# Value rows of four groups summed on TensorE through diagonals, in a block of attention and expert retrieval

## What is computed

```python
def _peer(xn, w_q, sub_keys, u_tab, v_tab):
    def body(xb):                                   # 128 tokens
        q = (xb @ w_q).reshape(128, 8 heads, 2, 128)
        sc = einsum('thpd,hpkd->thpk', q, sub_keys)
        s1, i1 = top_k(sc[:, :, 0], 16); s2, i2 = top_k(sc[:, :, 1], 16)
        top_s, pos = top_k(all 256 sums s1 + s2, 16)
        eidx = i1 * 128 + i2 at pos                 # 16 of 16384 experts
        g = softmax(top_s)
        hid = gelu(einsum('thkd,td->thk', u_tab[eidx], xb)) * g
        return einsum('thk,thkd->td', hid, v_tab[eidx])
h = h + _peer(rmsnorm(h)); out = rmsnorm(h)
```

## Time and profile before

| quantity | value |
|---|---|
| median of three runs | 1542.28 us |
| the profiled execution itself | 1541.62 us |
| its span, first to last instruction | 1539.8 us |
| mean granted TensorE clock | 0.939 of full speed |
| TensorE (PE) matmul busy | 1269.3 us, 82% |
| VectorE (DVE) busy | 1077.6 us, 70% |
| GpSimd (POOL) busy | 751.5 us, 49% |
| ScalarE (ACT) busy | 459.8 us, 30% |
| first dot to last add of the hosted stage | 110.06 to 529.7 us |

### The profile page before, as it was taken

The page is one execution under the profiler, slowest core; times in us unless marked ns, Lnnn a source line. Parts: engine busy times, 40 slices in busy tenths (PEclk is TensorE's granted clock), DMA queues, the critical chain, the costliest instruction groups (busy, mean ns, idle before and its releaser), DMA issues.

```text
span 1539.8 us, 13062 instructions
## 1 busy us (share of the span) xinstructions
PE 1269.3 (82%) x3727; PEld 658.2 (43%) x3727; DVE 1077.6 (70%) x2520; ACT 459.8 (30%) x1200; POOL 751.5 (49%) x637
## 2 busy tenths in 40 slices
PE   9999999988888488999787777677886787777778
PEld 7766655665545234444333333233332233332333
DVE  3247699999988867566666676666666766666654
ACT  3432355466343022222222222221222222222212
POOL 0016477675667443454544554445444554444440
PEclk9999999999989699999899999989999999999998
DMA  9669799997999999999999999999999999999995
GB/s 382 250 250 413 275 330 351 370 376 268 340 371 392 391 421 416 421 421 421 421 422 422 421 422 421 421 422 421 422 421 421 422 422 421 422 420 422 421 421 208
DMA packets 99741, 596.50 MB, mean 387 GB/s; under 512 B 11480, under 2 KB 11480, under 8 KB 42328
## 3 DMA queue, kind: packets, MB, share of 16 engines
q0 software_dynamic: 89856, 536.91, 86.0%
q1 hardware_dynamic: 9816, 58.77, 9.6%
HBM read 593.54 MB, written 2.10 MB: 387 GB/s over the span
## 4 chain that ended last, share of the span: by engine, by line
DMA 42%; PE 15%; DVE 6%; POOL 3%; issue 2%; ACT 2%; DVEq 0%; POOLq 0%
PE acc L994 13%; DMA map_mem<-in_peer_uv_dram,eidx 10%; DMA w_ring<-in_peer_uv_dram,eidx 9%; DMA v_all<-in_peer_uv_dram,eidx 7%; DMA act_mem<-in_peer_uv_dram,eidx 6%; DMA v_ring<-in_peer_uv_dram,eidx 3%; DMA mix_mem<-in_peer_uv_dram,eidx 3%; DMA u_ring<-in_peer_uv_dram,eidx 3%; DMA v_ring<-in_peer_v_dram,eidx 2%; PE mm L786 1%; ACT diag L1228 1%; DVE map_mem L1549 1%; DVE w_ring L1549 1%; PE sc L786 1%; POOL v_ring L692 1%
## 5 line engine op out<-in xcount | busy, mean ns | idle before, releaser
L1220 ACT ACTIVATE gel<-hid 128x4 f32<-128x4 f32 x126 | 25.8, 205 | 722.2 <-DVE hid L1549 712.5
L685 POOL DMA_INDIRECT u_ring<-in_peer_u_dram,eidx x112 | 136.8, 1221 | 172.9 <-DVE eidx L1529 99.5
L994 PE MATMUL acc<-v_all,diag 128*128 128x512 f32 x256 | 129.2, 651 | 61.1 <-ACT diag L1228 60.6
L692 POOL DMA_INDIRECT v_ring<-in_peer_v_dram,eidx x112 | 133.4, 1192 | 66.4 <-DVE h L1577 38.0
L1577 DVE SCALAR_TENSOR_TENSOR h<-v_ring,coef,h 128x1024 f32<-128x1024 f32 x112 | 143.9, 1284 | 14.3 <-DMA v_ring<-in_peer_v_dram,eidx 11.3
L994 PE MATMUL acc<-map_mem,diag 128*128 128x512 f32 x248 | 123.3, 644 | 32.0 <-ACT diag L1228 32.0
L994 PE MATMUL acc<-v_ring,diag 128*128 128x512 f32 x248 | 120.1, 629 | 32.3 <-ACT diag L1228 28.7
L1541 DVE CUSTOM_DVE_ANT_0 u_ring<-u_ring,hn 128x1024 f32<-128x1024 f32 x112 | 136.6, 1220 | 14.2 <-DMA u_ring<-in_peer_u_dram,eidx 14.0
L994 PE MATMUL acc<-u_ring,diag 128*128 128x512 f32 x248 | 119.1, 626 | 27.4 <-ACT diag L1228 25.8
L1228 ACT ACTIVATE diag<-ident,coef 128x128 f32<-128x128 f32 x392 | 126.3, 390 | 39.1 <-DVE coef L1567 30.8
L711 POOL DMA_INDIRECT v_all<-in_peer_uv_dram,eidx x64 | 76.1, 1189 | 92.3 <-PE acc L994 81.7
(11 more groups left out here) (281 smaller groups left out, 2331.9 us busy)
## 6 DMA issues: line engine op xcount, KB each, us to landing
w_ring<-in_slabs_dram SPq DMA_DIRECT2D x29, 1024.0 KB, 8.4
v_ring<-in_slabs_dram SPq DMA_DIRECT2D x6, 1024.0 KB, 11.2
u_ring<-in_slabs_dram SPq DMA_DIRECT2D x6, 1024.0 KB, 10.9
map_mem<-in_slabs_dram SPq DMA_DIRECT2D x6, 1024.0 KB, 7.9
h<-in_x_dram SPq DMA_DIRECT2D x4, 512.0 KB, 12.5
u_ring<-in_peer_u_dram,eidx POOLq DMA_INDIRECT x112, 6.9
v_ring<-in_peer_v_dram,eidx POOLq DMA_INDIRECT x112, 7.1
v_all<-in_x_cols_dram SPq DMA_DIRECT2D x3, 512.0 KB, 7.4
```

The lines of the kernel that those rows point to most:

```text
L685: nc.gpsimd.indirect_dma_start(out=u_ring[:, c % U_RING, :], out_offset=None, in_=peer_u[0], in_offset=bass.IndirectOffsetOnAxis(ap=eidx[n ...
L692: nc.gpsimd.indirect_dma_start(out=v_ring[:, c % V_RING, :], out_offset=None, in_=peer_v[0], in_offset=bass.IndirectOffsetOnAxis(ap=eidx[n ...
L994: last = nc.tensor.matmul(acc[half][:, :], diag[:, c % COLS, :], v_row(n, c)[:, half * BANK:(half + 1) * BANK], start=first, stop=(n % PH ...
L1220: nc.scalar.activation(gel[:, par, g0:g0 + COLS], hid[:, par, g0:g0 + COLS], ACT.Gelu).then_inc(gelu_done, 1)
```

## The change

Groups 5, 9, 13 and 17 (the tuple `SUMMED`) are no longer added row by row on VectorE. ScalarE makes four diagonals of their coefficients in a memory of their own (`sum_diag`, laid over the buffers `z_f` and `e_f` of the forget gate), TensorE multiplies each diagonal with its v row and accumulates the four rows in two banks of the rotation `mm`, one per 512 columns, and VectorE adds the two banks to `h` one slot later, or earlier if an `outproj` comes first. TensorE's part stands at gap 0 of slot k + 2, and the planner leaves room behind it (`SHARE_SUM` = 10.0). The adds of slots 7, 11, 15 and 19 fall away.

```diff
+SUMMED = (5, 9, 13, 17)
+SHARE_SUM = 10.0
...
     total, at = sum(share(p) for p in later), 0.0
+    total += SHARE_SUM * len(SUMMED)
+    summed_at = {(k + BEHIND) * GAPS: ("sum", k) for k in SUMMED}
     for p in later:
         k = int(at / total * (SLOTS - 1) * GAPS)
+        while summed_at and k >= min(summed_at):
+            slot = min(summed_at)
+            AFTER[slot].append(summed_at.pop(slot))
+            at += SHARE_SUM
+            k = int(at / total * (SLOTS - 1) * GAPS)
...
+        def row_taken(i):
+
+            if i // COLS in SUMMED and i % COLS == COLS - 1:
+                return mm_full, mm_done(("sum", i // COLS, 1))
+            return added, i + 1 - sum(COLS * k + COLS - 1 <= i for k in SUMMED)
...
             def gather_v(n, c):
                 if n or c >= V_RING:
-                    pool.wait_ge(added, TOPK * n + c + 1 - V_RING)
+                    pool.wait_ge(*row_taken(TOPK * n + c - V_RING))
...
+                elif kind == "sum":
+                    k, = p
+                    pe.wait_ge(*row_taken(COLS * k - 1))
+                    banks = [mm_bank((kind, k, half)) for half in range(2)]
+                    for c in range(COLS):
+                        pe.wait_ge(v_in[c % V_RING], 16 * (k * COLS // V_RING + 1))
+                        pe.wait_ge(sum_diag_done, COLS * SUMMED.index(k) + c + 1)
+                        for half in range(2):
+                            last = nc.tensor.matmul(banks[half][:, :], sum_diag[:, c, :], v_ring[:, c % V_RING, half * BANK:(half + 1) * BANK],
+                                                    start=(c == 0), stop=(c == COLS - 1))
...
+                elif kind == "sum":
+                    n, par, g0 = group_at(p[0])
+                    act.wait_ge(coef_done, p[0] + 1)
...
+                    for c in range(COLS):
+                        nc.scalar.activation(sum_diag[:, c, :], ident[:, :], ACT.Copy,
+                                             scale=coef[:, par, g0 + c:g0 + c + 1]).then_inc(sum_diag_done, 1)
...
                 elif kind == "outproj":
                     g, sl, t = p
+                    if sums_due:
+                        add_sum(sums_due.pop())
...
+            def add_sum(k):
+
+                for half in range(2):
+                    bk = mm_wait(("sum", k, half))
+                    hs = h[:, 0, half * BANK:(half + 1) * BANK]
+                    nc.vector.tensor_tensor(out=hs, in0=bk[:, :], in1=hs, op=ALU.add).then_inc(mm_drained, 1)
...
+                        if gap == 0 and k - BEHIND in SUMMED:
+                            coefs(*behind)
+                            sums_due.append(k - BEHIND)
+                        if gap == 1 and k - BEHIND - 1 in SUMMED and sums_due:
+                            add_sum(sums_due.pop())
...
-                        elif gap < GAPS - 1 and k >= BEHIND:
+                        elif gap < GAPS - 1 and k >= BEHIND and k - BEHIND not in SUMMED:
```

More of the change, by code:

```diff
@@ L303, in build @@
                 MM.append(("fturn", 0))
+        elif kind == "sum":
+            MM += [(*p, half) for half in range(2)]
         elif kind == "turn":
@@ L387, in build @@
         c_all = sb("c_all", [FH, SEQ])
-        z_f = sb("z_f", [FH, max_n])
-        e_f = sb("e_f", [FH, max_n])
+        gate_mem = sb("gate_mem", [P, 2 * max_n])
+        z_f = gate_mem[0:FH, 0:max_n]
+        e_f = gate_mem[0:FH, max_n:2 * max_n]
+        sum_diag = gate_mem[:, 0:COLS * P].rearrange("p (a n) -> p a n", a=COLS)
         selq = mix_mem[:, D:D + FH * P].rearrange("p (a b n) -> p a b n", a=FH // 2, b=2)
@@ L528, in build @@
         added = sem("added")
+        sum_diag_done = sem("sum_diag_done")
         v_used = sem("v_used")
@@ L707, in gather_row @@
                 elif place == FREE_ROWS + 2:
-                    pool.wait_ge(added, HOSTED)
+                    pool.wait_ge(*row_taken(HOSTED - 1))
                 elif place == RING:
@@ L838, in piece @@
                     last.then_inc(mm_full, 1)
+                elif kind == "sum":
[8 more added lines that the diff above has]
+                                                    start=(c == 0), stop=(c == COLS - 1))
+                            if c == COLS - 1:
+                                last.then_inc(mm_full, 1)
+                        if c < COLS - 1:
+                            last.then_inc(added, 1)
                 elif kind == "lamrow":
@@ L1155, in piece @@
                                              scale=rstd2[:, t:t + 1]).then_inc(mm_copied, 1)
+                elif kind == "sum":
+                    n, par, g0 = group_at(p[0])
+                    act.wait_ge(coef_done, p[0] + 1)
+                    if p[0] != SUMMED[0]:
+                        act.wait_ge(mm_full, mm_done((kind, SUMMED[SUMMED.index(p[0]) - 1], 1)))
+                    for c in range(COLS):
+                        nc.scalar.activation(sum_diag[:, c, :], ident[:, :], ACT.Copy,
+                                             scale=coef[:, par, g0 + c:g0 + c + 1]).then_inc(sum_diag_done, 1)
                 elif kind == "lambda":
@@ L1296, in _ @@
             handed = [0]
+            sums_due = []
             def link(ins):
@@ L1525, in topk_second @@
                         if n - 2 <= HOST_HEADS:
-                            dve.wait_ge(added, TOPK * (n - 2))
+                            dve.wait_ge(*row_taken(TOPK * (n - 2) - 1))
                         else:
@@ L1573, in add_row @@
                 dve.wait_ge(coef_done, GRP * n + c // COLS + 1)
-                if n or c:
-                    dve.wait_ge(added, TOPK * n + c)
+                before = (TOPK * n + c - 1) // COLS
+                if c % COLS == 0 and before in SUMMED:
+                    dve.wait_ge(*emptied(("sum", before, 1)))
+                elif n or c:
+                    dve.wait_ge(*row_taken(TOPK * n + c - 1))
                 ht = h[:, n // PH, :]
@@ L1608, in fin_tile @@
                 if t == 0:
-                    dve.wait_ge(added, HOSTED)
+                    dve.wait_ge(*row_taken(HOSTED - 1))
                 dve.wait_ge(v_used, PH * TOPK * (t + 1) - HOSTED)
```

## The result

The changed kernel takes 1592.39 us (median of 4 runs, 1588.97 to 1595.85) against 1542.01 before: a ratio of 1.032, 95% interval 1.0288 to 1.0352. It is 50 us slower, and outside the forecast of 1547 to 1582. The profiled execution took 1593.36 us with a span of 1591.5.

What follows compares the result with a forecast made beforehand. In the hosted stage VectorE and TensorE were taken as level up to 321 us, then VectorE leading. Lags of 7.7, 15.4, 21, 18.4, 21, 27 ended at +24 us on 1541.6, median 1566; range 1555 to 1581, 8 in 10 1547 to 1582.

Steps and rivals of the forecast that it cites:

- I take nothing: No gain counted from a fuller TensorE's clock, since the sums stand in stretches already full.
- the rival figure: If TensorE's clock stayed full up to 270 us, it would regain at most 5 us, giving 1561; no chance given.
- The planner's shift costs little before slot 5: Moving other pieces for the planner's room was taken as cheap there, since TensorE leads up to the forget gate.
- Step 3: Sum 13, entering at 321.8: last row lands 8.3 us after slot 14's last add, sum ends at 343, lag 21.
- Steps 1 and 2: Sums 5 and 9, at 223.0 and 270.5: each adds 7.7 us, lag 15.4 after both.
- Step 4: From the last FoX step to slot 19 VectorE leads with less work; lag falls from 21 to 18.4.
- Step 5: Slot 19: the last row's landing, remaining matmuls and scores delay slot 20 to 416; lag rises from 18.4 to 21.
- Step 6: Slot 20: `outproj` adds, the sum's adds and waits for the sum's bank raise the lag from 21 to 27.
- Step 7: Behind slot 20 the query stage moves, the awaited gelu stands ahead of the first query; 3 us back, to +24.
- faster: TensorE's sums fit its idle time by running 6.9 us ahead, winning VectorE's 15 us: 1527; chance 0.09.
- Level: VectorE, leading after 321 us with less work, pays the lag back to 6 to 8: about 1549; chance 0.16.
- Slower still: banks: Pieces behind every sum need a held bank, stopping TensorE 3.4 us more each, 14 in all: 1580; chance 0.13.

Runs made afterwards that it cites:

- early: Changed kernel with coefficients and diagonals of each sum made earlier, at gap 5 of the slot before; 1589.72 us, ratio 1.0312.
- extra: `shift` plus eight TensorE matmuls per sum on identity and a constant tile, waiting for nothing; VectorE still adds all rows; 1570.17 us.
- busy: Changed kernel with 14 small matmuls filling TensorE's wait for the diagonals; 1590.49 us, ratio 1.0308.
- shift: Kernel before with only the planner's room of four gaps of 10.0, no sums made; 1552.58 us, ratio 1.0054.
- half: Changed kernel with second and third row of each summed group multiplied in only 64 columns per bank; 1595.4 us, ratio 1.0343.
- noadd: Kernel before with VectorE's adds of groups 5, 9, 13 and 17 cut to 64 of 1024 columns; 1539.24 us, ratio 0.9986.
- early_rows: `early` with rows 2 and 3 of groups 5, 9, 13 (row 3 of 17) gathered into idle tiles outside the ring; 1590.53 us.
- early_later: `early` with TensorE's sum at gap 7 of its slot, behind the scores, instead of gap 0; 1569.34 us, ratio 1.0175.

## Why the prediction failed

The sign and the mechanism held, and half of the size was missing.

- **"It costs nothing but the first one's latency, 0.4 us per sum" failed.** I read ScalarE as half idle in every window (in one of the earlier trace rows it is busy 34.68 of 55 us) and priced its diagonals by duration. What counts is the queue ahead of the first one: 2.8, 1.4, 3.8 and 1.7 us from the coefficients' start to the diagonals' (221.84 to 224.63 at the first sum). TensorE waits 3.1, 3.7, 2.7 and 5.7 us where I had 0.8. ScalarE's share of busy time says nothing about what stands ahead of one instruction.
- **The wait for the coefficients was priced at the first sum alone**, and steps 2 to 5 have none. The sum's code also asks for VectorE's last add of slot k + 1, which the forecast doesn't name. TensorE arrived ahead of both at the second and the last sum. So 5.6 of the 15.2 us pass before the coefficients are there, and `early` could not win them: 1.56 and 5.10 us of waiting for that add are left in it.
- **"I take nothing" for the clock failed, with the wrong sign in the rival figure.** The granted clock fell to 0.81 and 0.86 in the windows of the first two sums (before: 0.95 and 1.00), and `extra`, with the same matmuls and no wait in front of them, has 1.00 in both; eight matmuls took 8.3 to 10.5 us instead of 6.9. The earlier trace rows had shown a low clock beside a gap; I used it for a gain only. The Trainium skill, "TensorE: Matmul & The Clock Gate", section "HAM oscillation", warns of idle gaps between bursts of matmuls. The trace agrees at the first sum, where a gap of 3.08 us stands in the window of 0.81; in `early` a gap of 3.23 us left the same window at 1.00. `busy` shows that a kept clock alone isn't the gain: 1590.5.
- **"The planner's shift costs little before slot 5" was right there and beside the point.** `shift` is 1.0 us late at slot 13, but 9.9 at slot 19. I didn't price the shift behind slot 16: 6.3 us to slot 19, as in `extra` (6.4) and the change (7.6).
- **Step 3, "8.3 us after that add", was mis-sized**: 11.4 us at the second sum in `half`, since a u row's gather of 1.54 us and its gap stand ahead on GpSimd. Late rows lay under the diagonals' wait, and came out in `early` (3.23 us for the third row) and `half`.
- **Steps 1 and 2, 7.7 us a sum**: for the matmuls alone 5.8 at slot 8 (`extra` less `shift`) and 8.9 for both at slot 13. So they add less than I thought, and the handoff the rest: 10.5 and 21.3.
- **Step 4, 2.6 us back by slot 19, didn't come**: the lag grew from 27.9 to 35.5, mostly the planner's.
- **Step 5, 2.6 us in slot 19, was 8.0.** It was not the row's landing: TensorE had been ready for 5.66 us when the diagonals came at 418.7, 3.65 of them before the coefficients were made, and its eight matmuls took 9.9 us.
- **Step 6, 6 us for the held banks, was right**: 6.5 from slot 20 to 21, and 6.6 in `extra`, which holds them too. **Step 7, 3 us back, didn't come**: +1.3.
- **Right**: TensorE leads, its rows in front of the scores are the loss (18 us net of the room), VectorE's relief is all but worthless (2 to 4 us), and the end of FoX costs VectorE 9.6 us (forecast 9). The waits name TensorE. Expected 5, 5 and 6 to 8 us in slots 7, 11 and 19; they are 10.7, 6.6 and 11.9.

Of the rivals, "faster" needed a TensorE that runs ahead; it does so only by 3 to 6 us, and spends that waiting for VectorE's add and for ScalarE. `noadd` shows that even a free sum would gain 2 to 3 us, not 15. "Level" needed VectorE to lead behind 321 us; there the lag grew instead, from 21.3 us at slot 13 to 51.3. "Slower still: banks" named a true wait, but only at the last sum.

Not settled: how the 26 us divide between diagonals, VectorE's last add, clock and rows; no kernel was run without the wait for that add. They lie over one another, so that removing one (`early`, `busy`, `half`, `early_rows`) showed the next (medians 3 us better to 3 worse), and the sum read from the waits (25.8) says what is seen, not what each removal returns. Nor do the runs say which moved piece makes the 6 us behind slot 16. No version here beats the kernel before; the best with sums is `early_later` at 1569.3, and `noadd`, without any cost of TensorE, gains 2 to 3 us with all other pieces where they were.

## To carry to other kernels

Before work is taken off a busy engine, cut it out there and time that: here, at nine tenths busy, a relief of 15 us was worth 2 to 3. That bounds every version of the idea that leaves the other pieces in their places. When an in-order engine gets a step that needs a fresh product of another engine, price the queue ahead of that product, every wait that its code sets, and the place of the step: moved behind what others wait for, the same work cost 10 us less, and 23 with the product made early. And when several waits end at one point, removing one of them shows only the next.

## What the hardware showed beside it

After a wait of 3.08 us TensorE's pairs of 128x512 matmuls took 2.04 us instead of 1.02, and came back to 1.02 after 5.1 us (225.16 to 230.25). A wait of 3.23 us in `early` was followed by 1.13 and 1.02, so the length of the wait alone doesn't decide; what does isn't shown. In `half`, with three waits and less work at the second sum, 0.58 was granted over 24 us, and the scores behind it took double time too: less work on TensorE was slower. Where ScalarE changes between exponential and gelu, a table load of 1.28 us stands in its queue (222.13); the run has 105 table loads, 50 of them ahead of a gelu, and the gate's exponentials and the gelu of the next group stand on either side of the diagonals. The Trainium skill, "ScalarE: Activation LUTs", section "What ACT_TABLE_LOAD costs", gives about 1.28 us for the load, which the trace confirms, and about 1.38 us more for a drain, which isn't seen here: the exponential starts at 223.43, 0.02 us behind the load.
